# State-space products of two steps at once in four tiles, an MLP loop written out: one kernel on one core

## The chip, the cores and the metric

The kernel runs on one core of one Trainium2 chip. The metric is the device time of one execution in microseconds (us), the median over runs. For this kernel a difference of 0.2%, about 4.9 us, is what a measurement can tell from no change. The engines are named as in the profile: PE is TensorE's matmuls and PEld its weight loads, DVE is VectorE, ACT is ScalarE, POOL is GpSimd, SP is SyncE, which issues the DMAs here.

## The reference

Two layers follow one another on x of 256 rows by 2048 (float32). The first is a gated delta network beside a Fourier branch, then an MLP; the second has three branches: spatial gating, a state-space branch and cross attention to a memory. The branch that the change touches is, cut down:

```
bu  = einsum('bsgh,gph->bsgp', u, b_bar)          # 64 groups g, 16 inputs h, 64 states p, complex
s_t = lam_bar * s_(t-1) + bu_t                    # scan over the 256 rows
y   = einsum('bsgp,ghp->bsgh', s, c_mat).real + d * u
y   = gelu(y); y = y * sigmoid(y @ glu_w + glu_b)
```

and the MLP of the first layer is `x + square(relu(h @ w_mlp_up)) @ w_mlp_down`.

## The kernel before

**The weight stream.** All large products are one stream of 396 units. A unit is a weight tile of 128 x 2048 floats (4 slices of 512 columns) that SP fetches into one of four buffers `raw`. For every unit ACT copies it rounded into `w_hi`, DVE writes the remainder `w_lo = raw - w_hi`, and PE does 24 matmuls of 128x512 (4 slices, 2 halves of the rows, 3 products: w_hi by a_hi, w_lo by a_hi, w_hi by a_lo; lines 2098 to 2100). ACT and DVE work two units ahead of PE: in slot n they split unit n + 2. DVE's split of unit n + 2 must be done when PE has finished unit n + 1.

**Work between units.** Everything else is cut into steps, and a table (`schedule`, line 165) puts each step at a place: place 2n is the middle of unit n on PE, place 2n + 1 its end. Each engine walks through the same places in its own queue, and does at a place its part of the step; semaphores tie the parts. Order on an engine is therefore fixed by the program; an engine that waits in a step holds back its own later splits.

**The state-space steps.** 16 steps (i = 0 to 15), each of 4 of the 64 groups in complex numbers, start 7 half-slots (3.5 units) apart (`SSM_PLACES`). Step i has four parts, at 0, 2, 3 and 5 half-slots:
- part 0: PE forms `bu` with four matmuls (2 real and imaginary, 2 groups of 32 partitions), each out of 32 rows of the array, into PSUM banks 0 and 1 (line 2385). DVE turns it with four multiplications `prod<-banks,rot` of 128x512 (lines 1844 to 1847), one operand in PSUM, one in SBUF.
- part 1: DVE adds (1850, 1851), both operands in SBUF, and scans (1857, four of them). On PE stands here the output product `y` of the step before (four matmuls, 32 columns of the array each, line 2398).
- part 2: four multiplications into `s_out` (1863 to 1866), and every second step one instruction on `y` (1878). Part 3: two more additions (1869, 1871).
- POOL makes the factors `rot` of step i + 2, ten instructions, once step i is finished on DVE: eight of 128x256 and two of 128x512 (lines 1222 to 1232).

Two steps are called a pair below: an even step and the odd one behind it, 7 units of the stream.

**The MLP loop.** The units 112 to 207 are run by every engine as a hardware loop of 3 turns of 32 units, with the waits counted by registers (`drive`, line 579).

Of the kernel before, what the change touches and what calls it, by code (L numbers as in the profile page):

```python
# [164 lines left out]
def schedule():  # L165
# [67 lines left out]
    put(end("w_mlp_up", 2 * p), "hidden", p, 0)  # L233
    put(end("w_mlp_up", 2 * p + 1), "hidden", p, 1)
# [48 lines left out]
LOOP0 = FIRST[INDEX[("w_mlp_up", 2)]]  # L283
LOOP_UNITS = 32
LOOPS = 3


class Side:
# [3 lines left out]
    def __init__(self, key, eng, sems, old, new):  # L292
        self.key, self.eng, self.sems, self.old, self.new = key, eng, sems, old, new
        self.count, self.it, self.per = 0, None, None
# [8 lines left out]
    def _in_loop(self, key, value):  # L303
        return value if self.it is None else value + self.it * self.per[key]

# [3 lines left out]
    def at(self, *names):  # L309

        marks = [self.old[n] if self.old else ("act", 1) for n in names]
        assert len({key for key, _ in marks}) == 1, names
        return self._in_loop(marks[0][0], max(value for _, value in marks))

    def here(self):

        assert self.count > 0
        return self._in_loop(self.key, self.count)
# [5 lines left out]
def build(nc, t_in, out, old, new):  # L324

    with ExitStack() as ctx:
# [90 lines left out]
        s_out = region("s_out", 0, [P, 2, 2, 2, T])  # L417
        prod = region("prod", 8, [P, 4, 2, T])
# [159 lines left out]
        def value(me, static, per):  # L578
            return static if me.it is None else static + me.it * per

        def drive(me, slot_work, after_loop):

            n = 0
            while n < UNITS:
                if n == LOOP0:
                    start = me.count
                    me.per = {k: v for k, v in (old or {}).get("per", {}).items()} if old else \
                        {"act": 0, "dve": 0, "pe": 0, "pool": 0}
                    with me.eng.Fori(0, LOOPS) as it:
                        me.it = it  # L590
                        for m in range(LOOP_UNITS):
                            slot_work(n + m)
                    me.it = None
                    per = me.count - start
                    new.setdefault("per", {})[me.key] = per
                    me.count += per * (LOOPS - 1)
                    for j in range(2):
                        for key, x in (("act", "hi"), ("dve", "lo")):
                            if me.key == key:
                                new[f"hidden{NPIECE - 2}.{j}.{x}"] = (key, me.count)  # L600
                                for k in range(NT):
                                    new[f"hidden{NPIECE - 2}.{j}.{k}.{x}"] = (key, me.count)
                    after_loop()
                    n += LOOPS * LOOP_UNITS
                    continue
                slot_work(n)
                n += 1

        def run_steps(me, steps, place):
            if 2 * LOOP0 <= place < 2 * (LOOP0 + LOOP_UNITS):  # L610
                local = (place - 2 * LOOP0 - 1) / 2
                for s, piece, j in ((4, 1, 0), (8, 1, 1), (20, 2, 0), (24, 2, 1)):
                    if local == s:
                        steps["hidden"](piece, j)
                return
# [12 lines left out]
        def _(sp):  # L628
            me = Side("sp", sp, done, old, new)

            def weight(n, it=None):

                if n >= RAW:
                    value = n - RAW + 1
                    sp.wait_ge(pe_used, value if it is None else value + it * LOOP_UNITS)
                if it is None:
                    src = t_in["w"][n]
                else:
                    src = t_in["w"][bass.ds(n + it * LOOP_UNITS, 1)].rearrange("a p n -> (a p) n")
                sp.dma_start(raw[:, n % RAW, :], src).then_inc(landed[n % RAW], 16)  # L640
# [141 lines left out]
            n = 0  # L782
            while n < UNITS:
                if n == LOOP0:
                    with sp.Fori(0, LOOPS) as it:
                        for m in range(LOOP_UNITS):
                            weight(n + m + RAW, it)
                    n += LOOPS * LOOP_UNITS
                    run_steps(me, steps, 2 * n)
                    run_steps(me, steps, 2 * n + 1)  # L790
                    continue
# [6 lines left out]
                n += 1  # L798
                if n != LOOP0 and n not in ends:
                    run_steps(me, steps, 2 * n)  # L800
                    run_steps(me, steps, 2 * n + 1)
# [8 lines left out]
        def _(act):  # L810
# [4 lines left out]
            def split(n):  # L815

                act.wait_ge(landed[n % RAW], value(me, 16 * (n // RAW + (n % RAW > 0)), 16 * LOOP_UNITS // RAW))
                if n >= HIGH:
                    act.wait_ge(pe_used, value(me, n - HIGH + 1, LOOP_UNITS))
# [9 lines left out]
            def job(tag, j):  # L829
# [9 lines left out]
                if mode == "square":  # L839
                    if ts_user[k] and me.it is None:  # L840
# [37 lines left out]
            def empty(i):  # L878
# [3 lines left out]
                act.wait_ge(pe_used, value(me, FIRST[i + 1], LOOP_UNITS))  # L882
                norm = "x" if i <= INDEX[("w_gate_a", 3)] else "mlp" if name == "w_mlp_up" else \
                    "mem" if name.startswith("xa_w") else "pre"
                if n == 0 and me.it is None:
# [160 lines left out]
            def ssm(i, part):  # L1046
# [1530 lines left out]
```

## Time and profile before

| | |
|---|---|
| median of 3 runs | 2452.07 us (2451.09 to 2452.88) |
| the profiled execution | 2454.28 us, its span 2452.5 us |
| PE / DVE / ACT / POOL busy | 99% / 63% / 42% / 11% of the span |
| state-space steps on PE | 1627.9 to 1978.5 us of the span |

The busy time of PE is modelled from pipelined matmuls, each shown with some 390 ns though the next one starts 227 ns behind it, so 99% means that it is never long without work, not that it runs at its peak. What can be shortened is read from the distance of starts. DVE's 63% is an average over the whole kernel; in the state-space steps it is much higher, and that stage is the one to read.

### The profile page before, as it was taken

The numbers are of one execution on the slowest core, as the hardware profiler recorded it, in microseconds if no ns is written. First come the engines' busy times: TensorE is split into PE (matmuls) and PEld (weight loads), VectorE is DVE, ScalarE is ACT, GpSimd is POOL, SyncE is SP. The second block draws the span as 40 slices with busy tenths as digits, with TensorE's granted clock in tenths as the row PEclk, the third lists the DMA queues.
The fourth block names the chain that finished last, engine by engine and source line by source line (L and its number), as shares of the span: only waits on it lengthen the run. The fifth ranks groups of instructions, "written<-read, shape, count | busy, mean of one in ns | idle before, by whom it ended". The sixth has DMA issues, their size and how long they took to land.

```text
span 2452.5 us, 31953 instructions
## 1 busy us (share of the span) xinstructions
PE 2429.2 (99%) x13482; PEld 1996.0 (81%) x13482; DVE 1534.6 (63%) x1530; ACT 1030.0 (42%) x860; POOL 274.8 (11%) x226
## 2 busy tenths in 40 slices
PE   8999999999999999999999999999999999999998
PEld 7888888878888888888888888887777778888886
DVE  6465556557676455445445567789999955446564
ACT  4553345334344443443443434443433444544332
POOL 1002201210000000000000000054556400000000
PEclk9999999999999999999999999999999999999999
DMA  6343354346755455555555555665555576566753
GB/s 257 135 164 115 136 184 168 108 149 245 262 193 184 177 189 190 188 189 191 186 191 194 187 196 205 224 242 192 189 187 194 187 284 234 173 240 227 257 197 137
DMA packets 84220, 475.10 MB, mean 194 GB/s; under 512 B 8704, under 2 KB 8832, under 8 KB 32512
## 3 DMA queue, kind: packets, MB, share of 16 engines
q1 hardware_dynamic: 84096, 473.32, 54.2%
q8 instruction: 94, 1.54, 0.2%
q14 instruction: 30, 0.25, 0.0%
HBM read 450.21 MB, written 23.07 MB: 193 GB/s over the span
## 4 chain that ended last, share of the span: by engine, by line
PE 96%; DMA 1%; DVE 1%; ACT 1%; issue 0%; SPq 0%; DVEq 0%; ACTq 0%
PE acc L2098 29%; PE acc L2100 29%; PE acc L2099 29%; PE banks L2262 3%; PE banks L2111 2%; PE banks L2318 1%; DMA raw<-in_w 1%; PE banks L2385 1%; PE banks L2398 1%; DVE w_lo L1272 0%; ACT w_hi L820 0%; DMA av<-spilled 0%; DVE stats L1324 0%; PE banks L2438 0%; PE banks L2420 0%; PE banks L2236 0%
## 5 line engine op out<-in xcount | busy, mean ns | idle before, releaser
L1272 DVE TENSOR_TENSOR w_lo<-raw,w_hi 128x2048 fp32r<-128x2048 f32 x394 | 908.1, 2308 | 552.7 <-ACT w_hi L820 551.5
L820 ACT ACTIVATE w_hi<-raw 128x2048 fp32r<-128x2048 f32 x394 | 751.8, 1914 | 591.0 <-DMA raw<-in_w 588.8
L2098 PE MATMUL acc<-w_hi,a_hi 128*128 128x512 f32 x2112 | 840.5, 398 | 5.8 <-DVE a_lo L1308 3.1
L2099 PE MATMUL acc<-w_lo,a_hi 128*128 128x512 f32 x2112 | 824.7, 390 | 0.0
L2100 PE MATMUL acc<-w_hi,a_lo 128*128 128x512 f32 x2112 | 824.4, 390 | 0.0
L2098 PEld LDWEIGHTS acc<-w_hi,a_hi 128*128 128x128 f32 x2112 | 397.3, 188 | 104.2 <-issue 15.3
L2100 PEld LDWEIGHTS acc<-w_hi,a_lo 128*128 128x128 f32 x2112 | 397.4, 188 | 84.9
L2099 PEld LDWEIGHTS acc<-w_lo,a_hi 128*128 128x128 f32 x2112 | 397.8, 188 | 78.5
L2098 PE MATMUL acc<-w_hi,b_hi 128*128 128x512 f32 x928 | 364.2, 392 | 0.0
L2100 PE MATMUL acc<-w_hi,b_lo 128*128 128x512 f32 x928 | 361.5, 390 | 0.0
L2099 PE MATMUL acc<-w_lo,b_hi 128*128 128x512 f32 x928 | 361.2, 389 | 0.0
L2100 PEld LDWEIGHTS acc<-w_hi,b_lo 128*128 128x128 f32 x928 | 174.2, 188 | 36.5
L2099 PEld LDWEIGHTS acc<-w_lo,b_hi 128*128 128x128 f32 x928 | 174.4, 188 | 35.3
L2098 PEld LDWEIGHTS acc<-w_hi,b_hi 128*128 128x128 f32 x928 | 174.3, 188 | 35.1
L1252 POOL MEMSET c_out<- 128x2048 f32 x1 | 1.8, 1810 | 1029.1 <-DMA spilled<-stage_b 1029.1
L907 ACT ACTIVATE stage<-acc,stats 128x512 f32<-128x512 f32 x72 | 45.6, 685 | 128.3 <-PE acc L2100 123.8
L1436 DVE TENSOR_TENSOR x_rows<-x_rows,acc 128x512 f32<-128x512 f32 x72 | 46.2, 683 | 39.0 <-PE acc L2100 39.0
L1222 POOL TENSOR_TENSOR rot<-pow_a,pow_b 128x256 f32<-128x256 f32 x32 | 47.5, 1486 | 175.9 <-DVE s_out L1871 130.6
L1857 DVE TENSOR_TENSOR_SCAN prod<-rad,prod 128x256 f32<-128x256 f32 x64 | 56.9, 948 | 0.6
L2098 PE MATMUL acc<-w_hi,m_hi 128*128 128x512 f32 x128 | 50.6, 395 | 0.0
L2099 PE MATMUL acc<-w_lo,m_hi 128*128 128x512 f32 x128 | 50.5, 395 | 0.0
L2100 PE MATMUL acc<-w_hi,m_lo 128*128 128x512 f32 x128 | 50.5, 394 | 0.0
(356 smaller groups left out, 1642.4 us busy)
## 6 DMA issues: line engine op xcount, KB each, us to landing
raw<-in_w SPq DMA_DIRECT2D x395, 1024.0 KB, 4.8
spilled<-stage SPq DMA_DIRECT2D x72, 256.0 KB, 6.0
gate_in<-spilled SPq DMA_DIRECT2D x20, 512.0 KB, 5.8
x_rows<-in_x SPq DMA_DIRECT2D x4, 512.0 KB, 8.2
x_rows<-in_x SPq DMA_DIRECT2D x1, 2048.0 KB, 9.2
mem_rows<-in_mem SPq DMA_DIRECT2D x2, 1024.0 KB, 5.8
spilled<-stage_b SPq DMA_DIRECT2D x8, 256.0 KB, 5.9
out<-y_rows SPq DMA_DIRECT2D x3, 512.0 KB, 2.7
```

Source lines behind the costliest of these rows:

```text
L820: act.activation(w_hi[:, n % HIGH, :], raw[:, n % RAW, :], ACT.Copy)\
L907: act.activation(dst, src, func, scale=rms(norm, t)).then_inc(act_emptied, 1)
L1222: pool.tensor_tensor(c_[:, g], pa[0][:, g], pb[0][:, g], ALU.mult).then_inc(pool_done, me.done())
L1272: dve.tensor_tensor(w_lo[:, n % RAW, :], raw[:, n % RAW, :], w_hi[:, n % HIGH, :].bitcast(F32), ALU.subtract).then_inc(lo_split, 1)
L1436: ins = dve.tensor_tensor(x_rows[:, t, cs], x_rows[:, t, cs], src, ALU.add)
L1857: dve.tensor_tensor_scan(pr[z + 1][:, g], r_, pr[z][:, g], 0.0, ALU.mult, ALU.add)\
L2098: pe.matmul(o, hi[:, tk], wh, start=first, stop=False)
L2099: pe.matmul(o, hi[:, tk], wl, start=False, stop=False)
L2100: ins = pe.matmul(o, lo[:, tk], wh, start=False, stop=last)
L2111: ins = pe.transpose(b[:, q * P:(q + 1) * P], src(q), ident)
L2262: ins = pe.matmul(b[rs, cs], lhs[rs, cs], rhs(k, rs), start=True, stop=True)
L2318: ins = pe.matmul(b(d, rs)[:, hd * P:(hd + 1) * P], lhs(d, t, rs, hd), rhs(d, rs, hd), start=True, stop=True)
```

## The change

**The products.** PE now forms `bu` of an even step and of the odd step behind it at once: eight matmuls, out of rows 0 to 31, 32 to 63, 64 to 95 and 96 to 127 of the array in turn, into all four PSUM banks. The output products of a pair come together too, eight matmuls into four column tiles. PE has nothing to do in the odd steps. **The inputs of the odd step** don't stay in PSUM: ACT copies banks 2 and 3 into a new SBUF tile `bu_odd` (two copies of 128x512, at part 0 of the even step), and DVE's four multiplications of the odd step read `bu_odd`. **State buffers:** `s_out` had two buffers, there are three now, since two steps are read at once. **The MLP loop** is written out; the places of its steps stay what they were, the register arithmetic goes.

```diff
@@ -230,8 +230,9 @@
     put(a + 6, "pre_root")
     p = NPIECE - 1
     put(end(f"w_mlp_down{p}", 2) - 2, "load_g_final")
-    put(end("w_mlp_up", 2 * p), "hidden", p, 0)
-    put(end("w_mlp_up", 2 * p + 1), "hidden", p, 1)
+    for p in range(1, NPIECE):
+        put(end("w_mlp_up", 2 * p), "hidden", p, 0)
+        put(end("w_mlp_up", 2 * p + 1), "hidden", p, 1)
...
-LOOP0 = FIRST[INDEX[("w_mlp_up", 2)]]
-LOOP_UNITS = 32
-LOOPS = 3
...
         s_out = region("s_out", 0, [P, 2, 2, 2, T])
+        s_third = region("s_third", 40, [P, 2, 2, T])
+        bu_odd = at("bu_odd", bb + 28 * KB, [P, 2, NW])
+        s_buf = lambda i: s_third if i % 3 == 2 else s_out[:, i % 3]
...
-                if n == LOOP0:
-                    start = me.count
-                    me.per = {k: v for k, v in (old or {}).get("per", {}).items()} if old else \
-                        {"act": 0, "dve": 0, "pe": 0, "pool": 0}
-                    with me.eng.Fori(0, LOOPS) as it:
-                        me.it = it
-                        for m in range(LOOP_UNITS):
-                            slot_work(n + m)
...
+        def drive(slot_work):
+            for n in range(UNITS):
                 slot_work(n)
...
+                if i < 16 and i % 2 == 0 and part == 0:
+                    act.wait_ge(pe_done, me.at(f"ssm{i}.bu"))
+                    act.wait_ge(dve_done, me.at(f"ssm{i - 1}.turned" if i else "ssm0.turned"))
+                    for g in range(2):
+                        act.activation(bu_odd[:, g], bank(2 + g), ACT.Copy).then_inc(act_done, me.done(f"ssm{i + 1}.taken"))
...
-                so = [s_out[:, k, z] for z in range(2)]
+                so = [s_buf(i)[:, z] for z in range(2)]
                 if i <= 15 and part == 0:
                     dve.wait_ge(pool_done, me.at(f"ssm{i}.rot"))
                     dve.wait_ge(dve_done, me.at("ssm.rad"))
-                    bu = [banks[:, 0:2, z * T:(z + 1) * T] for z in range(2)]
+                    bu = [(bu_odd if k else banks[:, 0:2])[:, :, z * T:(z + 1) * T] for z in range(2)]
                     if i == 0:
                         dve.wait_ge(pe_done, me.at("uT.3.T"))
                         dve.wait_ge(dve_done, me.at("ssm.pow"))
                     dve.wait_ge(dve_done, me.here())
-                    dve.wait_ge(pe_done, me.at(f"ssm{i}.bu"))
+                    if k:
+                        dve.wait_ge(act_done, me.at(f"ssm{i}.taken"))
+                    else:
+                        dve.wait_ge(pe_done, me.at(f"ssm{i}.bu"))
...
-                    if i >= 2:
-                        dve.wait_ge(pe_done, me.at(f"ssm{i - 1}.y"))
+                    if i >= 3:
+                        dve.wait_ge(pe_done, me.at(f"ssm{(i - 3) // 2 * 2 + 2}.y"))
...
-                if i <= 15 and part == 0:
-                    ct = i // 2
+                if i % 2:
+                    return
+                ct = i // 2
+                if i < 16 and part == 0:
                     pe.wait_ge(loaded["b_in"], 16)
                     pe.wait_ge(act_done, me.at("uT.3"))
                     if ct >= 2:
                         pe.wait_ge(act_done, me.at(f"gelu{ct - 2}"))
-                    b = [this_bank(g, f"bu{i}", g, f"ssm{i}.turned") for g in range(2)]
+                    b = [this_bank(q, f"bu{i}", q, f"ssm{i}.turned" if q < 2 else f"ssm{i + 1}.taken") for q in range(4)]
                     for z in range(2):
-                        for g in range(2):
-                            rs = slice(64 * (i % 2) + 32 * g, 64 * (i % 2) + 32 * g + 32)
-                            ins = pe.matmul(b[g][:, z * T:(z + 1) * T], b_in[rs, ct, z, :], uT[rs, ct, :],
-                                            start=True, stop=True)
+                        for q in range(4):
+                            ins = pe.matmul(b[q][:, z * T:(z + 1) * T], b_in[32 * q:32 * q + 32, ct, z, :],
+                                            uT[32 * q:32 * q + 32, ct, :], start=True, stop=True)
                     ins.then_inc(pe_done, me.done(f"ssm{i}.bu"))
-                if i >= 1 and part == 1:
-                    j = i - 1
-                    ct = j // 2
-                    pe.wait_ge(dve_done, me.at(f"ssm{j}.s", "ssm.c_out"))
-                    b = bank_of(f"ssy{ct}", 0)
-                    if j % 2 == 0:
-                        b = this_bank(2 + ct % 2, f"ssy{ct}", 0, f"ssm{2 * ct + 2}.ysum")
+                if i and part == 1:
+                    pe.wait_ge(dve_done, me.at(f"ssm{i - 1}.s", "ssm.c_out"))
+                    b = this_bank(2, f"ssy{ct - 1}", 0, f"ssm{i}.ysum")
                     for z in range(2):
-                        for g in range(2):
-                            rs = slice(64 * (j % 2) + 32 * g, 64 * (j % 2) + 32 * g + 32)
-                            ins = pe.matmul(b[rs, 0:T], c_out[:, z, 2 * j + g, :], s_out[:, j % 2, z, g, :],
-                                            start=z == 0, stop=z == 1)
+                        for q in range(4):
+                            j = i - 2 + q // 2
+                            ins = pe.matmul(b[32 * q:32 * q + 32, 0:T], c_out[:, z, 2 * j + q % 2, :],
+                                            s_buf(j)[:, z, q % 2, :], start=z == 0, stop=z == 1)
                     ins.then_inc(pe_done, me.done(f"ssm{i}.y"))
```

DVE's queue where an even step ends and an odd one begins, before (`prod` are the products of a step, `w_lo` a split of the stream):

```order
L1869 TENSOR_TENSOR s_out<-s_out,prod 128x512
L1871 TENSOR_TENSOR s_out<-s_out,prod 128x512
L1272 TENSOR_TENSOR w_lo<-raw,w_hi 128x2048
L1844 TENSOR_TENSOR prod<-banks,rot 128x512
L1845 TENSOR_TENSOR prod<-banks,rot 128x512
L1846 TENSOR_TENSOR prod<-banks,rot 128x512
L1847 TENSOR_TENSOR prod<-banks,rot 128x512
L1272 TENSOR_TENSOR w_lo<-raw,w_hi 128x2048
L1850 TENSOR_TENSOR prod<-prod 128x512
L1851 TENSOR_TENSOR prod<-prod 128x512
```

and the same place now:

```order
L1823 TENSOR_TENSOR s_third<-s_third,prod 128x512
L1825 TENSOR_TENSOR s_third<-s_third,prod 128x512
L1223 TENSOR_TENSOR w_lo<-raw,w_hi 128x2048
L1798 TENSOR_TENSOR prod<-bu_odd,rot 128x512
L1799 TENSOR_TENSOR prod<-bu_odd,rot 128x512
L1800 TENSOR_TENSOR prod<-bu_odd,rot 128x512
L1801 TENSOR_TENSOR prod<-bu_odd,rot 128x512
L1223 TENSOR_TENSOR w_lo<-raw,w_hi 128x2048
L1804 TENSOR_TENSOR prod<-prod 128x512
L1805 TENSOR_TENSOR prod<-prod 128x512
```

Nothing has moved on DVE; the four products of the odd step have another source, `bu_odd` in SBUF in place of `banks` in PSUM.

ACT's queue over the second and third of the pairs, now (`stage` is the emptying of a finished piece of the stream, `uT` the gelu of a finished pair):

```order
L770 ACTIVATE w_hi<-raw 128x2048
L1001 ACTIVATE bu_odd<-banks 128x512 x2
L770 ACTIVATE w_hi<-raw 128x2048 x3
L857 ACTIVATE stage<-acc,stats 128x512 x2
L770 ACTIVATE w_hi<-raw 128x2048 x4
L857 ACTIVATE stage<-acc,stats 128x512 x2
L1001 ACTIVATE bu_odd<-banks 128x512 x2
L770 ACTIVATE w_hi<-raw 128x2048 x2
```

The rows `bu_odd<-banks` are new: two copies a pair, each time ahead of a split of the stream.

PE's queue at an output product, now:

```order
L2047 MATMUL acc<-w_hi,a_lo 128x512
L2342 MATMUL banks<-s_third,c_out 32x256 x2
L2342 MATMUL banks<-s_out,c_out 32x256 x2
L2342 MATMUL banks<-s_third,c_out 32x256 x2
L2342 MATMUL banks<-s_out,c_out 32x256 x2
L2045 MATMUL acc<-w_hi,a_hi 128x512
```

Where four matmuls stood at two places (`L2398 MATMUL banks<-s_out,c_out 32x256 x4`), eight stand at one.

## Rows read from the trace of the kernel before

**Rows 1.** The page: PE, and the chain that ended last by engine.
```profile
PE 2429.2 (99%) x13482; PEld 1996.0 (81%) x13482; DVE 1534.6 (63%) x1530; ACT 1030.0 (42%) x860; POOL 274.8 (11%) x226
...
PE 96%; DMA 1%; DVE 1%; ACT 1%; issue 0%; SPq 0%; DVEq 0%; ACTq 0%
```
**Rows 2.** Waits of PE, whole span: total us, times, longest us.
```profile
PE acc L2098 <- DVE w_lo L1272: 2.4, 2, 1.9
```
**Rows 3.** Windows: stretch, us; busy us and count of each engine; clock, DMA.
```profile
968.20:1000.80 32.60, 32.60 (x145) 26.99 (x144) 14.85 (x8) 12.44 (x8) 0.00 (x0) 1.00 0.53 193
1334.40:1356.20 21.80, 21.80 (x97) 17.98 (x97) 9.02 (x4) 8.66 (x6) 0.00 (x0) 1.00 0.54 193
...
1757.40:1800.60 43.20, 43.20 (x201) 33.37 (x201) 40.43 (x41) 20.59 (x16) 25.40 (x21) 1.00 0.57 194
2008.00:2011.40 3.40, 3.40 (x9) 2.64 (x10) 3.37 (x3) 0.63 (x1) 0.00 (x0) 0.50 1.01 411
```
**Rows 4.** Timeline of PE around `bu`: start, duration (us), instruction.
```profile
1669.47 0.39 PE L2100 MATMUL acc<-w_hi,a_lo 128*128 128x512 f32 x1
1669.79 1.13 PE L2385 MATMUL banks<-uT,b_in 32*128 32x256 f32 x8
...
1671.19 0.39 PE L2099 MATMUL acc<-w_lo,a_hi 128*128 128x512 f32 x1
```
**Rows 5.** Timeline of PE around an output product.
```profile
1676.20 0.39 PE L2100 MATMUL acc<-w_hi,a_lo 128*128 128x512 f32 x1
1676.52 1.06 PE L2398 MATMUL banks<-s_out,c_out 128*32 128x256 f32 x8
...
1677.85 0.40 PE L2099 MATMUL acc<-w_lo,a_hi 128*128 128x512 f32 x1
```
**Rows 6.** Timeline of PE: as many matmuls on the whole array (cross attention).
```profile
2094.88 1.89 PE L2420 MATMUL banks<-kmT,xqT 128*128 128x256 f32 x8
```
**Rows 7.** Timeline of DVE over one pair, parts of it.
```profile
1768.65 0.69 DVE L1863 TENSOR_TENSOR s_out<-prod,rot 128x512 f32<-128x512 f32 x1
...
1771.46 2.28 DVE L1272 TENSOR_TENSOR w_lo<-raw,w_hi 128x2048 fp32r<-128x2048 f32 x1
...
1774.87 2.29 DVE L1272 TENSOR_TENSOR w_lo<-raw,w_hi 128x2048 fp32r<-128x2048 f32 x1
1779.00 0.69 DVE L1844 TENSOR_TENSOR prod<-banks,rot 128x512 f32<-128x512 f32 x1 [1.85 <-PE banks L2385]
...
1783.60 1.11 DVE L1850 TENSOR_TENSOR prod<-prod 128x512 f32<-128x512 f32 x1
...
1785.77 3.80 DVE L1857 TENSOR_TENSOR_SCAN prod<-rad,prod 128x256 f32<-128x256 f32 x4
...
1800.59 0.69 DVE L1844 TENSOR_TENSOR prod<-banks,rot 128x512 f32<-128x512 f32 x1 [0.81 <-PE banks L2385]
```
**Rows 8.** Timeline of DVE: four scans in a step where POOL had finished.
```profile
1700.57 2.44 DVE L1857 TENSOR_TENSOR_SCAN prod<-rad,prod 128x256 f32<-128x256 f32 x4
```
**Rows 9.** Timeline of POOL in the same pair.
```profile
1775.03 2.60 POOL L1222 TENSOR_TENSOR rot<-pow_a,pow_b 128x256 f32<-128x256 f32 x1 [7.54 <-DVE s_out L1871]
1777.59 0.61 POOL L1223 TENSOR_TENSOR ptmp<-pow_a,pow_b 128x256 f32<-128x256 f32 x1
...
1779.44 1.30 POOL L1225 TENSOR_TENSOR rot<-rot,ptmp 128x512 f32<-128x512 f32 x1
...
1784.13 1.06 POOL L1229 TENSOR_TENSOR rot<-pow_a,pow_b 128x256 f32<-128x256 f32 x1
```
**Rows 10.** Timeline of PE: where the unit split at 1771.46 begins.
```profile
1774.91 0.39 PE L2098 MATMUL acc<-w_hi,a_hi 128*128 128x512 f32 x1
```
**Rows 11.** The page: ACT's reading of PSUM banks, 128x512.
```profile
L907 ACT ACTIVATE stage<-acc,stats 128x512 f32<-128x512 f32 x72 | 45.6, 685 | 128.3 <-PE acc L2100 123.8
```

More of the change, by code:

```diff
@@ L312, in at @@
         assert len({key for key, _ in marks}) == 1, names
-        return self._in_loop(marks[0][0], max(value for _, value in marks))
+        return max(value for _, value in marks)
     def here(self):
         assert self.count > 0
-        return self._in_loop(self.key, self.count)
+        return self.count
 KB = 1024
@@ L781, in _ @@
             ends = {FIRST[i + 1] - 1: i for i in SPILLS}
[L782 to L791, printed above, removed]
+            for n in range(UNITS):
                 if n + RAW < UNITS:
@@ L797, in _ @@
                     run_steps(me, steps, 2 * n + 1)
[L798 to L801, printed above, removed]
+                if n + 1 not in ends:
+                    run_steps(me, steps, 2 * n + 2)
+                    run_steps(me, steps, 2 * n + 3)
             for t, n0, n1 in FINAL_DVE:
@@ L839, in job @@
                 if mode == "square":
-                    if ts_user[k] and me.it is None:
+                    if ts_user[k]:
                         act.wait_ge(dve_done, me.at(f"{ts_user[k]}.lo"))
@@ L881, in empty @@
                     return
-                act.wait_ge(pe_used, value(me, FIRST[i + 1], LOOP_UNITS))
+                act.wait_ge(pe_used, FIRST[i + 1])
                 norm = "x" if i <= INDEX[("w_gate_a", 3)] else "mlp" if name == "w_mlp_up" else \
                     "mem" if name.startswith("xa_w") else "pre"
-                if n == 0 and me.it is None:
+                if n == 0:
                     ready = {"w_f": "x.rinv", "w_mlp_up": "mlp.rinv", "xa_wv": "mem1.rinv"}.get(name)
@@ L1257, in _ @@
             for n in range(UNITS):
-                if not LOOP0 <= n < LOOP0 + LOOP_UNITS:
-                    run_steps(me, steps, 2 * n)
-                    run_steps(me, steps, 2 * n + 1)
+                run_steps(me, steps, 2 * n)
+                run_steps(me, steps, 2 * n + 1)
         @block.vector
@@ L1416, in empty @@
                     return
[L1417 to L1420 removed]
+                dve.wait_ge(pe_used, FIRST[i + 1])
+                if name[:10] == "w_mlp_down" or name == "w_o":
+                    dve.wait_ge(dve_emptied, emptied(i, "dve") - NT)
                 cs = slice(n * NW, (n + 1) * NW)
@@ L2040, in this_bank @@
                 new["bank"][(tag, j)] = i
-                if last_use[i] and me.it is None:
+                if last_use[i]:
                     pe.wait_ge(done[me.engine_of(last_use[i])], me.at(last_use[i]))
@@ L2048, in operand_ready @@
                 tag = {"w_f": "x", "w_o": "y", "w_mlp_up": "mlp", "w2_bx": "pre", "w_out": "merge"}.get(name)
-                if tag and me.it is None and (name != "w_f" or u >= EARLY):
+                if tag and (name != "w_f" or u >= EARLY):
                     pe.wait_ge(act_done, me.at(f"{tag}.{2 * u + 1}.hi"))
@@ L2069, in unit @@
                 if u == 0 and part == 0:
-                    if me.it is not None and n < LOOP0 + 8:
-                        pe.wait_ge(dve_emptied,
-                                   value(me, emptied(i - 2, "dve") - (NT if n == LOOP0 else 0), 8 * NT))
                     if i >= 2:
```

67 lines of the change are left out of this document (13 added, 54 removed).

## The prediction

> **What bounds the kernel now.** I read the page first: PE is never long without work, and the chain that ended last runs over PE for 96% [rows 1]. The waits of PE come next: it waited for DVE's split of the stream twice in the whole run, 2.4 us in all, 1.9 us the longest [rows 2]. So PE's queue is the bound, and a change can win time in two ways only: less on that queue, or none of those waits. It can lose time by making another engine late. Which engine is near to that is read from the window over one pair of state-space steps, 1757.4 to 1800.6: DVE is busy 40.43 of 43.20 us, ACT 20.59, POOL 25.40 [rows 3]. There DVE is nearly as full as PE, though the page gives it 63%.
>
> **The MLP loop.** PE starts 144 matmuls in 32.6 us in a stretch in which the loop turns, 0.226 us each, and 96 in 21.8 us behind the loop, where the code was straight before too, 0.227 us each [rows 3]. The two agree within the rounding of the windows, so the jump and the register work hide behind matmuls already queued. Written out, the same steps stand at the same places. I cost this half of the change at nothing, 1 us either way.
>
> **What PE saves.** A stream matmul starts 0.227 us behind the last. Around `bu` two starts lie 1.72 us apart (1669.47 to 1671.19) where two distances make 0.45: the insertion costs 1.27 us [rows 4]. The output product costs 1.65 less 0.45, 1.20 us [rows 5]. A whole pair shows the same and a little more: from 1757.41 to 1800.59 are 43.18 us, of which 7 units of 24 matmuls are 38.08, so two steps cost 5.10 us, 2.55 each [rows 3, 7].
>
> The eight records of four small matmuls take 1.13 us out of 32 rows [rows 4] and 1.89 us on the whole array [rows 6]: two neighbouring tiles run beside each other. Whether four do, no row shows. If they do, eight matmuls cost what four cost, and a pair costs PE 2.55 in place of 5.10: 40.63 us. If only two do, each of the two insertions grows by four more at the same rate, some 0.86 us: 42.4 us a pair. With 8 pairs the change would save 20.4 or 6.4 us, if PE were the only bound. I take four tiles. The Trainium skill (TensorE: Matmul & The Clock Gate, Part 3: Packing small matmuls) gives 3.07 times for four row tiles and 2.38 for three column tiles; by these figures it is nearer to 20 than to 6, and the rows agree as far as two tiles go.
>
> **What DVE then has to do.** A pair of 43.18 us holds 0.81 and 1.85 us in which DVE waits for PE's `bu` [rows 7], so DVE has 40.5 us of work. That is already PE's new 40.63. Now the work grows. POOL makes `rot` in the same stretch, and the two get in each other's way in a plain pattern. An instruction of DVE with both operands in SBUF takes 0.69 us alone and 1.11 us beside POOL [rows 7]; POOL's small instruction goes from 0.61 to 1.06 [rows 9]. Each lets the other in once, and one small POOL instruction costs DVE 0.42 to 0.43 us. Four scans take 2.44 alone [rows 8] and 3.80 with one small and one large POOL instruction between [rows 7]: 1.36 for both, so a large one costs 0.93. The products from PSUM are free of it: from 1779.00 on DVE runs them at full pace while POOL's large instruction takes its usual 1.30 [rows 7, 9].
>
> POOL's ten instructions of a step (eight small, two large) would cost DVE 8 x 0.43 + 2 x 0.93 = 5.3 us if all ran beside SBUF work. In the odd step before, only three small and one large did: two additions at 0.43 and the scans at 1.36, 2.2 us. The rest ran in DVE's wait of 1.85 us and under the four products from PSUM.
>
> The change takes away both covers in the odd step. Its four products read `bu_odd`, in SBUF, at the place where POOL has just begun, since the end of the even step releases it (1774.87, POOL starts at 1775.03) [rows 7, 9]; and the wait goes, because the input lies ready. So the odd step pays 5.3 in place of 2.2: 3.1 us more. In the even step the products still come from PSUM, but the wait of 0.81 us goes as well once DVE is late, and some one and a half small POOL instructions run beside SBUF work instead: 0.6 us. DVE's pair is 40.5 + 3.1 + 0.6 = 44.2 us. That is more than PE's 40.63, and 1.0 more than the 43.18 before. DVE sets the pace, by its splits.
>
> That the products from `bu_odd` are held by POOL is inferred from the additions; no row shows a multiplication of this form beside POOL. The Trainium skill (GPSIMD Engine Reference, § 8 Key points) says that POOL shares its SBUF interface with VectorE and contends with instructions of two SBUF inputs. By that rule the four products belong with the additions, which gives the 3.1 us; if the form of the operation decided, it would be 1.3. The rows agree with the rule for additions, scans and splits.
>
> **Over the stage.** DVE may be late by the slack of its tightest split: the one at 1771.46 ends 2.28 us later, at 1773.74, and PE begins its unit at 1774.91, so 1.2 us [rows 7, 10]. Seven pairs at 44.2 instead of 43.18: +7.1 us. Less the slack once: -1.2. In the last pair POOL has no step left to prepare; DVE catches up and PE runs at its own 40.63: -2.55. Sum **+3.4 us**.
>
> **ACT** gets two copies of 128x512 a pair at 0.69 us [rows 11], 1.3 us ahead of a split. With 20.6 of 43.2 us busy it has room; its split of that slot comes up to 1.3 us later, and DVE, which is then late itself, reads it later still. I take 0, with 0.9 a pair as the worst, most of it under DVE's lateness. The third state buffer only moves a wait that nobody had. DMA: no bytes are added; 0.
>
> **Two ends for the contention.** Below: the products of the odd step are free as before and only the lost wait counts, 3 small POOL instructions more (1.3 us), 42.4 us a pair. Above: large instructions at 1.2 and one more small one caught by a split, 44.8 us a pair. I take 44.2, nearest to the rows of the additions.
>
> **Clock.** Behind PE's one long wait, at 2008.0, PE was granted 0.50 of its clock for 3.4 us [rows 3], 1.2 GHz in place of 2.4, which costs 1.7 us of matmuls. PE would now wait some 3.6 us in each of 6 or 7 pairs. If the clock fell each time, most of the loss would lie in time in which PE waits for DVE anyway; what sticks out I put at up to 2.5 us for the stage.
>
> **The rivals.**
> - *Forecast: DVE sets the pace, +3.4 us.* Profiled 2454.28 + 3.4 = 2457.7. The median stands 2.2 below the profiled execution, so 2452.07 + 3.4 = **2455.5**. Its own range is 2452 to 2458. Chance 0.55.
> - *The products don't contend.* 42.4 us a pair: 7 x (42.4 - 43.18) - 1.2 - 2.55 = -9.2, so 2442.9. For it: a multiplication isn't an addition. Against it: splits, additions and scans all show it. Chance 0.18.
> - *PE stays the bound.* DVE's work stays below 40.6, because POOL's instructions fall elsewhere: all 20.4 us, 2431.7. It would need the wait that POOL used to be worth nothing. Chance 0.07.
> - *Slower for good: DVE at 44.8 and the clock beside it.* 7 x 1.6 - 1.2 - 2.55 = +7.5, and 1 to 2.5 for the clock: 2460.6 to 2462. The place is the split behind an even step; it decides from 44.5 us a pair on. Chance 0.20.
> - *Two tiles at a time only.* Then the change on PE isn't what it says, 42.4 a pair, still under DVE's 44.2; only the last pair shows it, +1.7: 2457.2. It is inside the forecast.
>
> **How the numbers follow.** A difference of 0.2% is 4.9 us, the least that can be told from none: 2447.2 to 2457.0. Faster: the second and third case, 0.25. Slower: the fourth and a fifth of the forecast's share, 0.31. The rest, 0.44, is no change. The range runs from the second case to the fourth, 2442.5 to 2461.5, and leaves out the third and the tail of the fourth.
>
> **What would show it.** In the profile after: the sixteen records of a pair's `bu` in about 1.1 us (two tiles at a time: 1.9 to 2.0); the distance of even steps 44.2 us (PE the bound: 40.6; no contention: 42.4); `prod<-bu_odd,rot` at 1.0 to 1.1 us on the mean; DVE's wait for `banks` near 0; and new waits of PE for `w_lo` in the stage, 15 to 25 us in all. Outside 1630 to 1980 us nothing should move. I am wrong if `prod<-bu_odd,rot` shows 0.69, or if the even steps come at 40.6.

## The result, and the profile after

| | before | after |
|---|---|---|
| median | 2452.6 us (8 runs, 2451.09 to 2453.99) | 2459.79 us (8 runs, 2456.82 to 2462.36) |
| ratio of the runs | | 1.0029, 95% interval 1.0018 to 1.0040 |
| the profiled execution | 2454.28 us, span 2452.5 | 2456.82 us, span 2455.0 |
| stage: start of `bu` of step 0 to the start of the last output product | 350.25 us | 355.46 us |

The change costs 7.2 us, 0.29%. The state-space steps are called the stage below. The page and the waits of PE, to be read against [rows 1, 2]:

```profile
PE 2408.5 (98%) x13482; PEld 1984.9 (81%) x13482; DVE 1563.3 (64%) x1530; ACT 1036.5 (42%) x876; POOL 334.3 (14%) x226
...
PE 81%; DVE 14%; issue 2%; DMA 1%; POOL 1%; ACT 1%; SPq 0%; DVEq 0%; ACTq 0%
...
PE acc L2045 <- DVE w_lo L1223: 26.0, 17, 2.7
```

The chain that ended last was 96% PE and 1% DVE; now 14% of it is DVE. PE waited twice for a split before, 2.4 us in all; now 17 times, 26.0 us. The same number of instructions keeps POOL busy for 334.3 in place of 274.8 us: it stands in instructions that it has started and can't finish. PE does what the change says. Here is one row of its timeline (start, duration, instruction) for each of two neighbouring pairs:

```profile
1753.50 1.15 PE L2333 MATMUL banks<-uT,b_in 32*128 32x256 f32 x16
...
1797.76 1.15 PE L2333 MATMUL banks<-uT,b_in 32*128 32x256 f32 x16
```

Sixteen records in 1.15 us, where eight took 1.13 [rows 4]: four tiles run at once. The two rows also show the pace: 44.26 us from pair to pair, where 43.18 stood before; the six distances behind the first are 44.19 to 44.30, 44.25 on the mean. The window over such a pair (busy us and count of PE, PEld, DVE, ACT, POOL; clock, DMA share, GB/s) shows who makes it, against [rows 3]:

```profile
1754.00:1798.30 44.30, 41.16 (x205) 32.39 (x205) 44.20 (x41) 20.87 (x17) 33.39 (x20) 1.00 0.55 186
```

DVE is busy for 44.20 of 44.30 us. And this is DVE's timeline through the odd step, with POOL's beside it, to be laid next to [rows 7, 9]:

```profile
1776.74 2.29 DVE L1223 TENSOR_TENSOR w_lo<-raw,w_hi 128x2048 fp32r<-128x2048 f32 x1
1778.94 0.69 DVE L1798 TENSOR_TENSOR prod<-bu_odd,rot 128x512 f32<-128x512 f32 x1
...
1781.35 2.29 DVE L1223 TENSOR_TENSOR w_lo<-raw,w_hi 128x2048 fp32r<-128x2048 f32 x1
1783.55 0.69 DVE L1804 TENSOR_TENSOR prod<-prod 128x512 f32<-128x512 f32 x1
1784.15 0.69 DVE L1805 TENSOR_TENSOR prod<-prod 128x512 f32<-128x512 f32 x1
1784.87 3.88 DVE L1811 TENSOR_TENSOR_SCAN prod<-rad,prod 128x256 f32<-128x256 f32 x4
1788.68 3.31 DVE L1223 TENSOR_TENSOR w_lo<-raw,w_hi 128x2048 fp32r<-128x2048 f32 x1
1791.92 1.10 DVE L1817 TENSOR_TENSOR s_out<-prod,rot 128x512 f32<-128x512 f32 x1
...
1796.03 3.38 DVE L1223 TENSOR_TENSOR w_lo<-raw,w_hi 128x2048 fp32r<-128x2048 f32 x1
```
```profile
1776.90 8.42 POOL L1174 TENSOR_TENSOR rot<-pow_a,pow_b 128x256 f32<-128x256 f32 x1 [6.96 <-DVE s_out L1825]
1785.28 1.00 POOL L1175 TENSOR_TENSOR ptmp<-pow_a,pow_b 128x256 f32<-128x256 f32 x1
...
1795.64 1.62 POOL L1184 TENSOR_TENSOR rot<-rot,ptmp 128x512 f32<-128x512 f32 x1
```

The products from `bu_odd` take 0.69 us, undisturbed. POOL's first instruction pays instead: it takes 8.42 us and ends 0.45 us into DVE's scans. From there the two take turns, and DVE pays at every instruction: scans 3.88 for 2.44, the split behind them 3.31 for 2.27, four products 1.10 for 0.69, the last split 3.38 for 2.28. That is 1.44 + 1.04 + 1.66 + 1.10 = **5.2 us in the odd step**, where it was 2.2 before. All ten instructions of POOL are in it: eight small ones at some 0.4 us each (in the scans and the products), and two large ones at 1.04 and 1.10 (in the splits). The even step pays a little more too:

```profile
1763.09 1.78 DVE L1804 TENSOR_TENSOR prod<-prod 128x512 f32<-128x512 f32 x1
1764.80 1.10 DVE L1805 TENSOR_TENSOR prod<-prod 128x512 f32<-128x512 f32 x1
1765.93 4.55 DVE L1811 TENSOR_TENSOR_SCAN prod<-rad,prod 128x256 f32<-128x256 f32 x4
```

1.09 + 0.41 + 2.11 = 3.6 us over the undisturbed times. Before it was 2.8, in a split, the two additions and the scans of the even step:

```profile
1759.81 2.54 DVE L1272 TENSOR_TENSOR w_lo<-raw,w_hi 128x2048 fp32r<-128x2048 f32 x1
1762.27 1.11 DVE L1850 TENSOR_TENSOR prod<-prod 128x512 f32<-128x512 f32 x1
1763.30 1.10 DVE L1851 TENSOR_TENSOR prod<-prod 128x512 f32<-128x512 f32 x1
1764.44 4.18 DVE L1857 TENSOR_TENSOR_SCAN prod<-rad,prod 128x256 f32<-128x256 f32 x4
```

Of the 7.2 us, 5.2 are in the stage. The last pair holds a part that I had not counted: behind its even step, PE still waits.

```profile
1952.67 0.50 PE L2045 MATMUL acc<-w_hi,a_hi 128*128 128x512 f32 x1 [2.54 <-DVE w_lo L1223]
```

Behind the stage the one long wait of PE, at the normalisation of the spatial gating (`sg_norm`), grew from 1.92 us (before, at 2007.88) to 2.73:

```profile
2011.36 0.50 PE L2045 MATMUL acc<-w_hi,a_hi 128*128 128x512 f32 x1 [2.73 <-DVE w_lo L1223]
```

### The profile page after: what moved, and what is told of

Same layout as the page of the kernel before. It is cut to its first block, busy times and chain, and to the rows that moved or that the text cites. A ratio compares the mean times of both kernels' runs of the same rounds, so it can differ in the third digit from the quotient of the medians.

```text
span 2455.0 us, 31452 instructions
## 1 busy us (share of the span) xinstructions
PE 2408.5 (98%) x13482; PEld 1984.9 (81%) x13482; DVE 1563.3 (64%) x1530; ACT 1036.5 (42%) x876; POOL 334.3 (14%) x226
## 4 chain that ended last, share of the span: by engine, by line
PE 81%; DVE 14%; issue 2%; DMA 1%; POOL 1%; ACT 1%; SPq 0%; DVEq 0%; ACTq 0%
PE acc L2045 24%; PE acc L2047 24%; PE acc L2046 24%; DVE w_lo L1223 5%; PE banks L2209 3%; DVE prod L1811 2%; PE banks L2058 2%; PE banks L2265 1%; DVE prod L1804 1%; DMA raw<-in_w 1%; DVE prod L1818 1%; DVE prod L1805 0%; DVE prod L1820 0%; DVE prod L1798 0%; DVE prod L1801 0%
## 5 line engine op out<-in xcount | busy, mean ns | idle before, releaser
L1223 DVE TENSOR_TENSOR w_lo<-raw,w_hi 128x2048 fp32r<-128x2048 f32 x394 | 920.9, 2341 | 550.3 <-ACT w_hi L770 549.2
L1174 POOL TENSOR_TENSOR rot<-pow_a,pow_b 128x256 f32<-128x256 f32 x32 | 92.9, 2902 | 125.7 <-DVE s_out L1825 59.4
L857 ACT ACTIVATE stage<-acc,stats 128x512 f32<-128x512 f32 x72 | 45.6, 684 | 119.0 <-PE acc L2047 118.9
L1811 DVE TENSOR_TENSOR_SCAN prod<-rad,prod 128x256 f32<-128x256 f32 x64 | 64.0, 1058 | 0.6
```

What stands on the lines that cost most here:

```text
L857: act.activation(dst, src, func, scale=rms(norm, t)).then_inc(act_emptied, 1)
L1174: pool.tensor_tensor(c_[:, g], pa[0][:, g], pb[0][:, g], ALU.mult).then_inc(pool_done, me.done())
L1223: dve.tensor_tensor(w_lo[:, n % RAW, :], raw[:, n % RAW, :], w_hi[:, n % HIGH, :].bitcast(F32), ALU.subtract).then_inc(lo_split, 1)
L1811: dve.tensor_tensor_scan(pr[z + 1][:, g], r_, pr[z][:, g], 0.0, ALU.mult, ALU.add)\
```

## The experiments

Columns of the windows are as above. Every ratio is to runs of the kernel before, taken beside it on the same chip.

**1. The loop alone.** The kernel before, with the hunks of the MLP loop taken over and nothing else.

```diff
-                if n == LOOP0:
-                    with me.eng.Fori(0, LOOPS) as it:
+            for n in range(UNITS):
+                slot_work(n)
```

> The kernel before with only the MLP loop written out; the state-space part is untouched. Theory (all of the loss is in the state-space stage): 2452.6 us, within 1 us, and the pairs at 43.18 us as before. Rival (the written-out code costs something in fetching instructions or in the places of the steps): between 2453.6 us and the 2459.8 us of the changed kernel.

Measured: 2452.85 us, ratio 1.0002 (0.9993 to 1.0011), the state-space steps at 21.59 us each as before, and the stage at 350.25 us. The written-out loop costs nothing that can be measured; all of the loss is in the other half of the change.

**2 and 3. POOL taken away.** In both kernels POOL makes `rot` for steps 0 and 1 only, and the later steps use these two again, so what is computed is no longer the reference.

```diff
-                if i > 15 or part:
+                if i > 1 or part:
                     return
...
-                    dve.wait_ge(pool_done, me.at(f"ssm{i}.rot"))
+                    dve.wait_ge(pool_done, me.at(f"ssm{i % 2}.rot"))
```

> The changed kernel, in which POOL computes rot for the first two steps only and all later steps use those two again (so the phases of steps 2 to 15 are left out of the computation); nothing else is taken away. Theory (POOL's twenty instructions of a pair cost DVE about 10.6 us there, and that alone makes DVE the pace): DVE falls to some 34 us of work a pair, PE no longer waits for w_lo, the even steps come every 40.6 us, and the time is 2459.8 less 7 x (44.25 - 40.63), about 25 us, less: 2434 us, between 2430 and 2437. Rival (the pace is made by DVE's own longer list, by ACT's copies ahead of a split, or by the order of the places): the pairs stay above 43 us and the time above 2450 us.

> The kernel before with the same piece left out: rot is computed for steps 0 and 1 only. Theory (before, PE was the bound and DVE's lost time lay beside it): no gain, 2452.6 us within 1.5 us, pairs at 43.18 us; DVE's waits for PE grow by what POOL no longer takes. Rival (contention already cost the kernel before something): more than 2 us faster.

Measured: the changed kernel without POOL's work 2434.84 us, ratio 0.9932 (0.9916 to 0.9947); the kernel before without it 2450.99 us, ratio 0.9996 (0.9987 to 1.0006). First a pair of the changed kernel without that work, from `bu` to `bu`:

```profile
1747.98 1.15 PE L2333 MATMUL banks<-uT,b_in 32*128 32x256 f32 x16
...
1788.63 1.15 PE L2333 MATMUL banks<-uT,b_in 32*128 32x256 f32 x16
...
1748.00:1788.60 40.60, 40.60 (x201) 32.50 (x200) 36.19 (x41) 20.99 (x17) 0.00 (x0) 1.00 0.58 199
```

A pair comes every 40.65 us, so PE does save 2.5 us a pair (40.63 was worked out); DVE has 36.19 us to do (some 34 was expected) and time to spare. The same piece left out is worth 25 us in the changed kernel. In the one before it is worth nothing in the stage, 350.25 us with and without; the medians differ by 1.6 us, which is not clear of noise (the interval holds 1). So POOL's work beside DVE is what keeps the gain back in the stage, and it costs something only once DVE is the bound. The rival, that DVE's longer list or ACT's copies set the pace, is refuted: both are still there.

**4. The odd step's products from PSUM.** The copy goes; `y` moves to bank 0, which the even step's products have released by then.

```diff
-                    bu = [(bu_odd if k else banks[:, 0:2])[:, :, z * T:(z + 1) * T] for z in range(2)]
+                    bu = [banks[:, 2 * k:2 * k + 2, z * T:(z + 1) * T] for z in range(2)]
...
-                    b = this_bank(2, f"ssy{ct - 1}", 0, f"ssm{i}.ysum")
+                    b = this_bank(0, f"ssy{ct - 1}", 0, f"ssm{i}.ysum")
```

> The changed kernel without ACT's copy: the four products of the odd step read their PSUM banks 2 and 3 directly, and the output product of the pair goes to bank 0, which the even step's products have released. Nothing is left out. Theory (POOL can work only beside DVE instructions that do not hold both operands in SBUF; four products from PSUM let three small and one large instruction of POOL through, 3 x 0.43 + 0.93 = 2.2 us): DVE falls from 44.25 to 42.0 us a pair, time 2459.8 - 7 x 2.2 = 2444 us, between 2441 and 2447. Rival 1 (the products from bu_odd took 0.69 us in the trace, so reading them from SBUF costs nothing and it is the lost wait of 1.85 us alone): no change, 2459 to 2460 us. Rival 2 (the output product now waits for the even step's products on bank 0 and holds PE up): slower than 2460 us.

Measured: 2444.29 us, ratio 0.9967 (0.9955 to 0.9979). The second distance is PE's own 40.65 us; from the fourth on the pairs come every 42.3 us. The window over one of them, and the timelines of DVE and POOL in the odd step:

```profile
1790.20:1832.50 42.30, 40.93 (x202) 32.39 (x201) 42.20 (x41) 16.06 (x11) 30.39 (x20) 1.00 0.57 199
```
```profile
1814.11 0.68 DVE L1789 TENSOR_TENSOR prod<-banks,rot 128x512 f32<-128x512 f32 x1
...
1820.02 4.57 DVE L1802 TENSOR_TENSOR_SCAN prod<-rad,prod 128x256 f32<-128x256 f32 x4
```
```profile
1812.07 2.60 POOL L1168 TENSOR_TENSOR rot<-pow_a,pow_b 128x256 f32<-128x256 f32 x1 [5.63 <-DVE s_third L1816]
1814.64 0.62 POOL L1169 TENSOR_TENSOR ptmp<-pow_a,pow_b 128x256 f32<-128x256 f32 x1
1815.22 0.62 POOL L1168 TENSOR_TENSOR rot<-pow_a,pow_b 128x256 f32<-128x256 f32 x1
1815.80 0.62 POOL L1169 TENSOR_TENSOR ptmp<-pow_a,pow_b 128x256 f32<-128x256 f32 x1
1816.50 4.65 POOL L1171 TENSOR_TENSOR rot<-rot,ptmp 128x512 f32<-128x512 f32 x1
```

The product itself lasts 0.68 us against 0.69 from `bu_odd`: as seen from DVE, nothing has changed. As seen from POOL everything has: its first instruction ends 0.56 us into the first product from PSUM, in 2.60 in place of 8.42 us, and three more run at their own 0.62 beside the products. Where an operand lies is paid for by the other engine first, and comes back later: 1.9 us a pair from the fourth on, 15.5 us in the stage (339.98 against 355.46) and as much in the median. The copy to SBUF turned a gain of 8 us into a loss of 7.

**5. One gap in DVE's run.** To see what POOL's 8.42 us wait for, one wait is put behind the first product from `bu_odd`.

```diff
                     dve.tensor_tensor(pr[0], bu[0], c_, ALU.mult).then_inc(dve_done, me.done())
+                    if k:
+                        dve.wait_ge(dve_done, me.here())
```

> The changed kernel with one wait more on DVE: behind the first of the four products from bu_odd it waits for that product's own end before it starts the second, so that its back-to-back run of SBUF instructions has one gap. Nothing is left out. Theory (POOL gets the port at a gap of DVE's run, and then the two take turns until POOL is done; the sum of what POOL takes is the same wherever that begins): POOL's first instruction of an odd step ends 5 us earlier, at 3 us in place of 8.4; the second to fourth product rise from 0.69 to about 1.1 us, and the scans of the odd step get cheaper by as much; the pair stays at 44.3 to 44.4 us and the time at 2460 to 2461 us. Rival (POOL's start is not decided by gaps): the products stay at 0.69 us and POOL's first instruction at 8.4 us.

Measured: 2459.19 us, ratio 1.0027 (1.0017 to 1.0038), against 2458.97 for the changed kernel on the same chip. DVE's four products, its scans and its last split of the odd step, and POOL's first instruction:

```profile
1779.48 0.68 DVE L1798 TENSOR_TENSOR prod<-bu_odd,rot 128x512 f32<-128x512 f32 x1
1780.20 0.99 DVE L1801 TENSOR_TENSOR prod<-bu_odd,rot 128x512 f32<-128x512 f32 x1
1781.11 1.10 DVE L1802 TENSOR_TENSOR prod<-bu_odd,rot 128x512 f32<-128x512 f32 x1
1782.14 1.10 DVE L1803 TENSOR_TENSOR prod<-bu_odd,rot 128x512 f32<-128x512 f32 x1
...
1788.64 4.55 DVE L1813 TENSOR_TENSOR_SCAN prod<-rad,prod 128x256 f32<-128x256 f32 x4
...
1797.70 2.28 DVE L1223 TENSOR_TENSOR w_lo<-raw,w_hi 128x2048 fp32r<-128x2048 f32 x1
```
```profile
1777.44 3.21 POOL L1174 TENSOR_TENSOR rot<-pow_a,pow_b 128x256 f32<-128x256 f32 x1 [5.63 <-DVE s_out L1827]
```

A gap of 0.04 us (1780.16 to 1780.20) lets POOL in: its instruction takes 3.21 in place of 8.42 us, the products behind the gap take 0.99 to 1.10, and in return the step's last split is back at 2.28. I had expected the scans to get cheaper; they did not (4.55, against 3.88), it was the work behind them that did, back at 0.68 a product. The pair is 44.1 us, the time the same within noise, if 0.8 us under what I expected. As long as POOL's instructions fall beside SBUF work of DVE, their sum does not depend on which of it they meet.

**6. The changed kernel once more.**

> The changed kernel as it is, once more, for a second profiled execution: the first showed no stretch at half clock, and its time was the lowest of eight. Theory (the mean of the pairs is fixed, and what varies between executions is in which of PE's waits the clock falls): pairs again at 44.25 us, one or more stretches of 3.4 us at 0.50 behind waits of PE in the stage or after it, and 1 to 1.7 us of time for each. Rival (the spread comes from the pairs themselves): pairs that differ from 44.25 us by more than 0.2.

Measured: 2458.97 us, ratio 1.0030 (1.0020 to 1.0040); its profiled execution 2458.76 us, pairs from 44.16 to 44.30 us. The pairs are the same, as expected. Stretches at half clock in the stage or right behind it, which I expected, there were none in this trace either. It has one at the same early place as the kernel before (at 100.5 us), which the first trace of the changed kernel lacked.

**7 and 8. Pairs further apart.** If DVE sets the pace, PE can be given more of the stream beside it: six pairs 15 half-slots apart in place of 14, in the changed kernel and in that with the direct products.

```diff
-            put_at(2 * (a + 3) + 1 + SSM_PLACES * i + place, "ssm", i, part)
+            put_at(2 * (a + 3) + 1 + SSM_PLACES * i + min(i // 2, EXTRA) + place, "ssm", i, part)
-    a += 3 + -(-SSM_PLACES * 17 // 2)
+    a += 3 + -(-(SSM_PLACES * 17 + EXTRA) // 2)
```

> The changed kernel with the state-space steps further apart: the first six distances of a pair are 15 places in place of 14 (7.5 units of the stream in place of 7), what follows starts three units later. Nothing is left out. Theory (DVE sets the pace with 44.25 us a pair, so another half unit lets it take in only one more half split, 1.15 us, while PE gets 2.72 us more of its own work beside it): PE's part of a pair is 43.4 us, DVE's 45.4, PE waits 2.0 in place of 3.6 us, six times 1.6 us won: 2450 us, between 2447 and 2453. Rival (the pair's distance is set by a chain of waits between PE, ACT and DVE that the places only move): 2459 to 2461 us.

> Both edits: the odd step's products read PSUM directly, and six pairs lie 15 places apart. Nothing is left out. Theory: DVE has 42.35 + 1.15 = 43.5 us in a spaced pair, PE 40.65 + 2.72 = 43.4, so PE waits for w_lo for less than 0.5 us a pair where it waited 1.7: six times 1.6 us less than the kernel with the direct products alone (2444.3): 2435 us, between 2433 and 2438. Rival (contention grows with the place shift, since POOL's instructions now meet other work of DVE in every second pair): 2440 to 2445 us.

Measured: 2462.87 us, ratio 1.0044 (1.0031 to 1.0058), and 2449.64 us, ratio 0.9987 (0.9978 to 0.9996). Both miss, 13 and 15 us above what I expected, and the second is worse than the direct products alone. The waits of PE in the second, and two windows, the first up to 4.2 us into the longest wait (it runs from 2170.3 to 2182.5), the other from 6.7 us before its end on:

```profile
PE banks L2050 <- DVE xqT L1892: 12.2, 1, 12.2
...
PE acc L2037 <- DVE w_lo L1218: 4.5, 5, 1.3
```
```profile
2160.00:2174.50 14.50, 10.30 (x46) 8.26 (x44) 0.00 (x0) 4.98 (x6) 0.00 (x0) 1.00 0.48 161
2175.80:2189.20 13.40, 5.56 (x15) 4.23 (x16) 9.09 (x5) 2.40 (x2) 0.00 (x0) 0.50 0.37 145
```

PE's waits for splits fell from 10.2 us in 7 (run 4) to 4.5 in 5. But what follows the stage stands three units later now, and at the end of the cross attention the load of its gate, `xg_rows`, was issued behind the place where DVE needs it: DVE waited 22.3 us for it and PE 12.2. In that wait, from 2175.6 on, PE was granted 0.50 of its clock (1.2 GHz), and kept it for 6.7 us of its matmuls behind the wait, which cost some 3.3 us.

With the 16.3 us that three units take PE taken off, the stage gained 7.4 us in run 7 and 5.4 in run 8, where 9.6 was expected of each, and what lies behind the stage lost some 12 us in each. So the larger part of the miss was made behind the stage, and a smaller one in it. In run 7 the stage holds two stretches of 3.4 us at 0.50, behind waits of 2.40 and 2.48 us, and the two pairs with them took 47.7 and 47.8 us in place of 45.4.

**9 and 10. The same without that collision.** Four pairs widened, and the four heads of the cross attention 5 places apart in place of 6.

```diff
-EXTRA = 6
+EXTRA = 4
...
-        put(a + 4 + 3 * h, "xa_score", h)
-        put(a + 5 + 3 * h, "xa_prob", h)
-        put(a + 6 + 3 * h, "xa_out", h)
+        put_at(2 * a + 9 + 5 * h, "xa_score", h)
+        put_at(2 * a + 11 + 5 * h, "xa_prob", h)
+        put_at(2 * a + 13 + 5 * h, "xa_out", h)
...
-    put(a + 16, "load_xg")
+    put_at(2 * a + 29, "load_xg")
```

> Direct products and a wider spacing as in the kernel with both edits before, but four pairs in place of six are widened by one place, and the four heads of the cross attention stand five places apart in place of six, so that the load of xg_rows is issued no later than in the kernel before (there it came two units too late, and PE waited 12.2 us for what it feeds). Nothing is left out. Theory (the miss of the widened kernels was made behind the stage, not in it): the wait of 12.2 us and the 13.7 us of PE at half clock behind it are gone, and in the stage PE waits some 1.4 us less in each of four pairs than with the direct products alone: 2444.3 - 5.6 = 2439 us, between 2436 and 2441. Rival (the wider spacing itself loses, whatever comes behind): 2444 us or more.

> The changed kernel with only that spacing: four pairs widened by one place, heads five places apart, the products still from bu_odd. Nothing is left out. Theory (DVE sets the pace, each widened pair lets PE do 2.72 us of the stream beside 1.15 us of DVE's): 4 x 1.57 = 6.3 us less than the changed kernel, 2459.4 - 6.3 = 2453 us, between 2451 and 2455. Rival (spacing does nothing for a stage in which DVE sets the pace): 2459 us.

Measured: with the direct products **2434.39 us, ratio 0.9926 (0.9912 to 0.9939)**, 18 us faster than the kernel before; with `bu_odd` 2449.14 us, ratio 0.9986 (0.9977 to 0.9995). With the late load out of the way both gain, and both came out some 4 us better than expected. In the first I can name them. Against run 4, and again less the two units, the stage is 4.0 us shorter (5.6 was expected) and what lies behind it 4.3 us: PE's wait at `sg_norm`, 2.4 us in run 4, is gone, since `av` had landed before DVE asked for it, and so is the stretch of 3.4 us at half clock that stood behind it there, 1.7 us of PE's work. The nearer heads were not tried by themselves, so what they do beside moving the load stays open. Its waits of PE for splits:

```profile
PE acc L2037 <- DVE w_lo L1218: 4.3, 4, 1.3
```

This version beats both kernels and stands level with the changed kernel without POOL's work (2434.84 us), by a sum of two things: less the two units its stage is 5.6 us longer than there (346.86 - 10.88 against 330.34), and what follows is 4.4 us shorter.

## Why the prediction was right, and where it was not

The forecast case was the one that happened (DVE sets the pace, 44.2 us a pair, a small loss), and the time, 2459.79, lies inside the range, 4.3 us above the 2455.5 predicted. It lies outside the 2452 to 2458 that I gave this case by itself, and above 2457.0, from where I called a change slower; slower had 0.31 and no change 0.44. Of the 4.3 us, 1.8 were made in the stage, 0.5 come from the kernel before, whose median over eight runs is 2452.6, and 2.0 are not in the stage as the traces show it. The steps:

- **The loop at nothing:** right, 1.0002 (run 1).
- **PE saves 2.55 us a pair, four tiles:** right. 16 records in 1.15 us, and 40.65 us a pair as soon as POOL is out of the way (run 2), 2.52 less than before.
- **DVE's pair of 44.2 us:** right in size. Predicted were 5.3 us for a whole step of POOL's instructions; 5.2 were measured, out of 2.2, and made up as predicted, eight small instructions and two large ones. The even step was put at 0.6 more and measured at 0.8.
- **The products from `bu_odd` at 1.0 to 1.1 us:** wrong. They show 0.69, by which I had said that I would be wrong. The step that failed is "the four products belong with the additions", read as where the price is paid. POOL doesn't share each instruction; it is kept out of a run of DVE that has no gap, and then gets all of its turns later in the same step. Run 5 makes the gap, and the products show 0.99 to 1.10 at the same total. What I had right is that SBUF products take POOL's cover away (run 4: 1.9 us a pair). By my own sign I was wrong on where the cost shows, and right on its sum, which needed only that each of POOL's ten instructions meets SBUF work somewhere in the step.
- **DVE's wait for `banks` near 0, PE's waits of 15 to 25 us in the stage:** right. The first is gone; the second is 22.2 us in 14 waits. The 26.0 us above are those of the whole run.
- **Seven pairs +7.1, slack -1.2, last pair -2.55, in sum +3.4:** the sum is near because two errors go against each other. The first two terms, put at +5.9, came to +4.2: six distances at 44.25 are +6.5, the first distance, 39.6 against 41.9, is -2.3. Seven pairs at 44.25 would be +7.6, so the slack was 3.4 us in place of 1.2; I had read it from one split in the middle of the stage, and why the start has more was not looked into. The last term failed. I reasoned that in the last pair POOL has nothing to prepare; but `rot` of step 15 is made beside step 14, at the head of the last pair, and DVE enters that pair late. From its `bu` to the last output product it takes 50.3 us, against 49.3 before: +1.0 in place of -2.55, and the stage +5.2 in place of +3.4. Without POOL's work the last pair does take 46.8 us, 2.5 less than before (run 2).
- **ACT at nothing:** right. DVE is busy for 44.20 of 44.30 us, so it doesn't wait for a copy; with the copies and without POOL the pair is 40.65 us.
- **The clock, up to 2.5 us in the stage:** not seen in either trace of the changed kernel. In the profiled executions the whole difference was 2.5 us, because the one before held two stretches of 3.4 us at 0.50 (at 100.0 and 2008.0, 1.7 us of matmuls each) and the one after none but that at the end, which every trace has; the second execution of the changed kernel, whose stage starts at the same time as before (1627.7 against 1627.9), stands 4.5 us above it. The mean granted clock of whole executions is 0.9976 over 45 runs of the kernel before and 0.9962 over 16 of the changed one, at 2452.6 and 2459.6 us on the mean. A 3.4 us stretch at 0.50 takes 0.0007 off that mean, so the changed kernel has about two more of them in an execution. That this is the remaining 2 us of the median, beyond the 5.2 of the stage, would fit, but was not shown: those executions left no trace. Run 5 speaks against a full 1.7 us for each: its trace has three such stretches, two of them in the stage, and took 2458.75 us, as long as the second trace of the changed kernel with one, 2458.76. The first of the two (from 1839.1) lies in a pair of 45.4 us; the next pair was 43.0, so most of it was given back by a shorter wait. The second (from 1927.8) lies in a pair of 45.6 us. What the clock costs the median stays open.

The Trainium skill (GPSIMD Engine Reference, § 8 Key points) names the shared SBUF interface and the instructions of two SBUF inputs. Runs 2 and 4 agree with it; that a whole run of such instructions keeps POOL out, and a gap of 0.04 us lets it in, is what the traces add.

**The rivals.** Products that don't contend (42.4 us a pair, 2442.9): refuted as an account of this kernel, though its 42.4 us a pair is what run 4 shows (42.3), where the products read PSUM. PE as the bound: refuted. DVE at 44.8 with the clock beside it: the pairs stay at 44.26, so its mechanism did not decide, though its time of 2460.6 was nearer than the forecast's; that is luck. Two tiles only: refuted by the 1.15 us.

## What to carry to other kernels

Before you take work off the engine that bounds a stage, add up the second engine's work in that stage with its waits removed: here 40.5 of 43.2 us, and the waits that went were time in which POOL had done part of its work undisturbed. A copy from PSUM to SBUF that costs nothing on the engine that makes it can still cost, here 15.5 us: the cover that a PSUM operand gave to GpSimd is gone, and the price appears behind it, on instructions that the change didn't touch. When steps are moved further apart, look at what the whole table behind them loads and needs: in run 8 three units cost 12 us two hundred microseconds later, while the stage itself had gained 5.4.

## What the runs showed of the hardware

- DVE's instructions with both operands in SBUF, started back to back (0.60 us apart at 0.69 each), kept one POOL instruction, 0.62 us elsewhere, for 8.42 us, through the one under way and seven more, and it ended 0.45 us into the scans. In run 5 a gap of 0.04 us behind the first product let it in, and from then on the two engines took turns: 0.41 us of DVE's time for a POOL instruction of 128x256, 1.0 to 1.1 us for one of 128x512.
- Not every such turn needs a gap: at 1760.87 of the changed kernel POOL's large instruction, asked for as DVE's split began, was served behind that one split (the addition after it took 1.78 us). In run 4 the same instruction, asked for as a split began too (1816.50), waited through the split and the two additions behind it (4.65 us). What tells these cases apart stays open.
- Four row tiles of 32x128, fp32: four records start within 0.02 us, the next four 0.32 us later, and each four after them 0.22 us behind the last; sixteen take 1.15 us, where eight in two tiles took 1.13.
- In a wait of PE of 12.2 us (run 8) the clock was still at 1.00 for the first 5.3 us, then at 0.50 for the other 6.9 us and for 6.7 us of matmuls behind it. Behind the wait of 1.92 us before it stood at 0.50 for 3.4 us [rows 3]. Behind fourteen waits of 0.5 to 2.7 us in the stage it did not fall at all in either trace of the changed kernel, but it fell for 3.4 us at two waits of 2.6 us in run 5 and at two of 2.4 and 2.5 us in run 7. The length of the wait alone does not tell them apart.
